# A transformer block on one core: the last two groups of the down projection issued as one

## The reference, cut to what matters

```python
for l in range(DEPTH):                       # DEPTH = 1, x is (1, 1024, 1024) float32
    h = rms_norm(x, g_mix[l])
    ...                                      # attention and mLSTM heads give mix
    x = x + mix @ w_out[l]
    h2 = rms_norm(x, g_ffn[l])
    x = x + (silu(h2 @ w_gate[l]) * (h2 @ w_up[l])) @ w_down[l]     # D_FF = 2816
```

## Time and profile before

| | |
|---|---|
| median of 3 runs | 1052.51 us (1050.98 to 1052.51) |
| the profiled execution, its own time | 1053.27 us |
| its span, first to last instruction | 1051.5 us |
| PE busy | 1022.6 us (97%) |
| DVE, POOL, ACT busy | 683.3, 707.2, 432.0 us |
| mean granted clock of TensorE | 0.988 |

### The profile page before, as it was taken

How to read it: one execution, slowest core, us unless ns; L and a number is a source line. 1 busy time by engine, 2 the same in 40 slices (tenths; PEclk the granted TensorE clock), 3 DMA queues, 4 the chain that set the end, 5 groups by cost and what they waited for, 6 DMA issues and landing times.

```text
span 1051.5 us, 13511 instructions
## 1 busy us (share of the span) xinstructions
PE 1022.6 (97%) x4970; PEld 841.0 (80%) x4970; DVE 683.3 (65%) x790; ACT 432.0 (41%) x895; POOL 707.2 (67%) x555
## 2 busy tenths in 40 slices
PE   9999999999989997999999999999999999999978
PEld 7898878878878876888888888888888888888856
DVE  4259359857752579474858676675858585766386
ACT  7545124357740556533434252434334342524420
POOL 0138578825655337978778687786887786878872
PEclk9999999999999998999999999999999999999988
DMA  7123212131032001111211212112112112121104
GB/s 232 56 61 89 72 41 61 61 130 32 21 122 60 20 11 51 60 50 41 81 41 44 78 41 66 55 41 80 40 41 81 41 50 72 41 70 51 41 30 160
DMA packets 71162, 66.06 MB, mean 63 GB/s; under 512 B 5305, under 2 KB 53689, under 8 KB 71097
## 3 DMA queue, kind: packets, MB, share of 16 engines
q1 hardware_dynamic: 70104, 64.71, 19.8%
q10 hardware_dynamic: 992, 0.49, 0.2%
HBM read 60.48 MB, written 4.21 MB: 62 GB/s over the span
## 4 chain that ended last, share of the span: by engine, by line
PE 73%; DVE 17%; issue 4%; ACT 3%; POOL 2%; DMA 0%; POOLq 0%; SPq 0%; DVEq 0%; ACTq 0%
PE banks L759 23%; PE banks L761 22%; PE banks L760 22%; DVE af_lo L1905 7%; DVE af_raw L1896 2%; DVE af_raw L1898 2%; ACT prob L1391 1%; PE banks L779 1%; DVE sg L1884 1%; PE banks L845 1%; POOL wr_lo L698 1%; DVE af_raw L1887 1%; DVE af_raw L1901 1%; DVE prob L1828 1%; DVE smx L1833 1%
## 5 line engine op out<-in xcount | busy, mean ns | idle before, releaser
L698 POOL TENSOR_TENSOR wr_lo<-wr_raw,wr_hi 128x512 fp32r<-128x512 f32 x231 | 315.0, 1392 | 38.4 <-ACT wr_hi L1221 33.3
L692 POOL TENSOR_TENSOR wr_raw<-wr_raw,wr_raw 128x512 f32<-128x512 f32 x132 | 191.0, 1451 | 130.0 <-PE banks L761 115.4
L759 PE MATMUL banks<-hf_hi,wr_hi 128*128 128x512 f32 x616 | 243.0, 394 | 6.9 <-issue 2.7
L761 PE MATMUL banks<-hf_hi,wr_lo 128*128 128x512 f32 x616 | 241.5, 392 | 0.0
L760 PE MATMUL banks<-hf_lo,wr_hi 128*128 128x512 f32 x616 | 241.3, 392 | 0.0
L1983 DVE TENSOR_TENSOR x<-banks,x 128x1024 f32<-128x1024 f32 x154 | 188.2, 1224 | 61.4 <-PE banks L761 46.5
L1221 ACT ACTIVATE wr_hi<-wr_raw 128x512 fp32r<-128x512 f32 x231 | 136.9, 625 | 159.4 <-POOL wr_raw L692 101.5
L759 PE MATMUL banks<-w_hi,actT_hi 128*128 128x512 f32 (+1 forms) x448 | 173.1, 386 | 1.5 <-DVE x L1792 1.5
L760 PE MATMUL banks<-w_lo,actT_hi 128*128 128x512 f32 (+1 forms) x448 | 168.6, 376 | 0.0
L761 PE MATMUL banks<-w_hi,actT_lo 128*128 128x512 f32 (+1 forms) x448 | 168.5, 376 | 0.0
L759 PEld LDWEIGHTS banks<-hf_hi,wr_hi 128*128 128x128 f32 x616 | 116.4, 189 | 36.2 <-DVE sg L1884 4.4
(11 more groups left out here) (201 smaller groups left out, 1236.1 us busy)
## 6 DMA issues: line engine op xcount, KB each, us to landing
wr_raw<-in_w_up SPq DMA_DIRECT2D x46, 256.0 KB, 3.4
wr_raw<-in_w_gate SPq DMA_DIRECT2D x44, 256.0 KB, 3.3
wr_raw<-in_w_down SPq DMA_DIRECT2D x44, 256.0 KB, 3.1
w_raw<-in_w_in SPq DMA_DIRECT2D x32, 256.0 KB, 3.5
w_raw<-in_w_out SPq DMA_DIRECT2D x16, 256.0 KB, 2.6
x<-in_x SPq DMA_DIRECT2D x8, 512.0 KB, 6.2
out<-x SPq DMA_DIRECT2D x16, 256.0 KB, 2.2
x_in<-in_x SPq DMA_DIRECT2D x7, 512.0 KB, 4.3
```

The source lines that it names most:

```text
L692: nc.gpsimd.tensor_tensor(wr_raw[slot(q, f)][:, :], wr_raw[slot(q, a)][:, :], wr_raw[slot(q, b)][:, :], ALU.subtract).then_inc(wsum, 1)
L698: nc.gpsimd.tensor_tensor(wr_lo[s][:, :], wr_raw[s][:, :], wr_hi[s][:, :].bitcast(F32), ALU.subtract).then_inc(wf_lo, 1)
L759: nc.tensor.matmul(ps, x_hi, wh, start=first, stop=False, skip_group_check=more)
L761: return nc.tensor.matmul(ps, x_lo, wh, start=False, stop=last, skip_group_check=more)
```

## The change

Five things change, all in the last two down stages, down 9 (QA) and down 10 (QB).

The order of TensorE: products are issued as 1 of QA, 2 of QA, 1 of QB, 2 of QB, and then form by form, QA's and QB's product of a form behind each other (`LAST_PRODUCTS`, `down_pair`). Both accumulate in the same banks and VectorE adds them once, so 14 adds of 128x1024 go; the last form is added bank by bank (`dve_last`).

The place of QB's weights: seven slots of their own, in space of the normalised tokens' forms 6 and 5, which no product reads any more once forms 6 and 5 of up 10 are done. Their loads and sums wait for that instead of for slots.

The low parts of the last activations: made by VectorE between its adds, not by GpSimd at the end; those of forms 1 and 2 in a place of their own, ahead of the sums.

The order of ScalarE and GpSimd in these two stages: hand-written lists that alternate QA and QB (`LAST_HIGH`, `LAST_LOWS`, `LAST_SUMS`), with functions that give each its count.

The stores: the last four wait for one add each.

```diff
+        DEAD6 = [M0 + 2 * SIDE, M0 + 2 * SIDE + SLOT, W0 + 2 * SIDE, W0 + 2 * SIDE + SLOT]
+        DEAD5 = [M0 + 3 * SIDE, M0 + 3 * SIDE + SLOT, M1]
+        LAST_LOW = M1 + SLOT
...
+        first_dead = len(UPPER + LOWER)
+        SLOTS.append({f: first_dead + i for i, f in enumerate((1, 2, 7, 3, 5, 6, 4))})
...
+        LAST_PRODUCTS = [(QA, 1), (QA, 2), (QB, 1), (QB, 2)] + [(q, f) for f in FORMS[2:] for q in (QA, QB)]
...
         def slot_free(engine, q, f):
+            if q == QB:
+                engine.wait_ge(gu_done, product(GU["up", JS - 1], 5 if f in (5, 6, 4) else 6))
...
+            def down_pair(j):
+                for q, f in LAST_PRODUCTS:
+                    n, b = at_form(f), q - QA
+                    first = {1: 0, 6: 0, 7: 0, 4: 0}.get(f, 4)
+                    pe.wait_ge(wf_lo, low_count(q, f))
+                    pe.wait_ge(act_lo_s, 7 * (j + b) + n + 1)
+                    s = slot(q, f)
+                    new = b == 0 and f in (1, 2, 5)
+                    for t in range(4):
+                        if b == 0 and t % 2 == 0:
+                            if n >= 2:
+                                pe.wait_ge(down_add, 14 * j + 2 * n - 3 + t // 2)
...
+                        last = three(bank[first + t][:, :], af_hi[b][f][:, a], af_lo[b][f][:, a],
+                                     wr_hi[s][:, :], wr_lo[s][:, :], new, b == 1, f not in (1, 2, 5))
+                        if b == 1 and (t % 2 == 1 or f == FORMS[-1]):
+                            last.then_inc(dn_done, 1)
...
+            def act_last():
+                for q, f in LAST_HIGH[2:7]:
+                    weight_high(q, f)
+                for f in A_HI[:3]:
+                    act_high(JS - 1, {1: 1, 2: 2, 4: 4}[f])
...
+            def dve_last(j):
+                act_low(JS - 1, 1)
+                act_sums(JS - 1, 1)
+                dve.wait_ge(act_raw, 8 * JS)
+                for n, f in enumerate(FORMS[:-1]):
+                    add_down(j, n, f)
+                    if n + 2 < len(FORMS):
+                        act_low(JS - 1, FORMS[n + 2])
+                dve.wait_ge(down_add, 14 * j + 12)
+                for t in range(4):
+                    dve.wait_ge(dn_done, 14 * j + 12 + t + 1)
+                    xs = x1[:, 4 + t, 0:N]
+                    V_.tensor_tensor(xs, bank[t][:, :], xs, ALU.add).then_inc(down_add, 1)
```

More of the change, by code:

```diff
@@ L614, in _ @@
             for t in range(4):
-                store(4 + t, 0, 13 + t // 2)
+                store(4 + t, 0, 13 + t)
             sp.wait_ge(out_s, 16 * 2 * T)
@@ L707, in fourth_sum @@
                                         ALU.subtract).then_inc(h2_s4, 1)
-            for q in range(NQ):
+            for q in range(QA):
                 n = 16 * (q // 2 + 1)
@@ L746, in _ @@
                     block_low(q, f)
[L747 to L752, removed]
+            for q in (QA, QB):
+                n = 16 * (q // 2 + 1)
+                pool.wait_ge(b11_s[q % 2], n)
+                pool.wait_ge(b12_s[q % 2], n)
+                block_sum(q, 5, 7, 1)
+                pool.wait_ge(wsum, sum_count(q, 5))
+                block_low(q, 1)
+                pool.wait_ge(b22_s[q % 2], n)
+                block_sum(q, 6, 3, 5)
+                pool.wait_ge(wsum, sum_count(q, 6))
+                pool.wait_ge(b21_s[q % 2], n)
+                block_sum(q, 4, 2, 6)
+                pool.wait_ge(wsum, sum_count(q, 4))
+                block_low(q, 2)
+            for f in (6, 5):
+                block_low(QA, f)
+                block_low(QB, f)
+            for q in (QA, QB):
+                block_sum(q, 7, 3, 7)
+            pool.wait_ge(wsum, sum_count(QB, 7))
+            for f in (7, 3, 4):
+                block_low(QA, f)
+                block_low(QB, f)
         @block.tensor
@@ L1501, in act_down @@
             def act_down(q, j):
[L1502 to L1507, removed]
+                for f in FORMS:
+                    weight_high(q + 1, f)
             act_first()
@@ L1516, in _ @@
                     act_up(q, j)
-                else:
+                elif q < QA:
                     act_down(q, j)
+                elif q == QA:
+                    act_last()
         @block.vector
@@ L1969, in dve_first, with add_down @@
                 gated(0, 0, 2, af_raw[0][2])
+            def add_down(j, n, f):
+                rows = 0 if f in (1, 2, 6, 3) else 4
+                half = {1: 0, 2: 0, 6: 1, 3: 1, 5: 1, 7: 1, 4: 0}[f]
+                first = 0 if f in (1, 6, 7, 4) else 2
+                for h in range(2):
+                    dve.wait_ge(dn_done, 14 * j + 2 * n + h + 1)
+                    if n >= 1 or j >= 1:
+                        dve.wait_ge(down_add, 14 * j + 2 * n + h - 1)
+                    xs = x1[:, rows + 2 * h:rows + 2 * h + 2, half * N:(half + 1) * N]
+                    V_.tensor_tensor(xs, banks[first + h][:, :, :], xs, ALU.add).then_inc(down_add, 1)
             def dve_down(j):
[L1972 to L1973 removed]
                 for n, f in enumerate(FORMS):
[L1975 to L1978, removed]
[L1979 to L1983 removed]
+                    add_down(j, n, f)
[4 more added lines that the diff above has]
+                for n, f in enumerate(FORMS[:-1]):
+                    add_down(j, n, f)
+                    if n + 2 < len(FORMS):
[5 more added lines that the diff above has]
+                    V_.tensor_tensor(xs, bank[t][:, :], xs, ALU.add).then_inc(down_add, 1)
             dve_first()
```

68 lines of the change are left out of this document (52 added, 16 removed).

## The result

The changed kernel takes 1039.89 us (median of 4 runs, 1039.06 to 1041.04), the kernel before 1051.98 us in the same comparison (4 runs). The ratio is 0.9885, 95% interval 0.9874 to 0.9897: 12.1 us less. Forecast were 1041.6 and a range of 1039.2 to 1044.5. The profiled execution took 1039.53 us, its span is 1037.7.

A forecast was written before the change was run, and what follows sets the result against it. PE, busy 97% of the span, was taken as the bound. Last matmul end at 1037.1 plus a 3.5 us tail gave 1040.6 against 1051.5, 10.9 us less; forecast median 1041.6 us, range 1039.2 to 1044.5.

The forecast's parts named there:

- The two old waits: TensorE's waits in down 9 and 10, 2.2 and 4.9 us, would go, with half clocks costing 1.7 and 2.3.
- The new wait: TensorE waits for VectorE ahead of the fifth and sixth products, 1.4 us in all, bounds 0 and 3.0.
- rival A: The forecast itself for the whole kernel: 1041.6 us, own range 1040.3 to 1043.0, chance 0.60.
- rival C: VectorE keeps up because GpSimd gives it more turns than priced: 1.4 us less, 1040.2, chance 0.12.
- What 168 matmuls need: Joined down 9 and 10 take 0.230 us per matmul, 167 steps from 996.91, ending at 1035.7 without waits.
- The new wait ahead of the fifth product: TensorE waits 1.1 us for VectorE's first add, behind low parts, a gate product and four sums taking 11.1 us.
- The clock behind the new wait: Waits of 1.1 and 0.3 us in the joined stages cause no clock loss; a drop would cost 1.7 us.
- Rival B: The clock falls behind the new wait in the joined stages: 1.7 us more, 1043.3, chance 0.15.
- The weights in time: Down 10's loads start at 986.1, GpSimd's first sum at 994.3; weights arrive before use, smallest slack 2.7 us.
- Rivals D and E: A weight or activation part late, 1044.5 to 1048, chance 0.08; down 10's loads not early, slower than before, chance 0.02.
- GpSimd rid of seven low parts: GpSimd drops seven low parts, 8.7 us, the first being what TensorE waited 4.9 us for.
- The tail: From last matmul to end of span, a one-bank add and single store take 3.5 us instead of 4.45.

The follow-up runs named there:

- operands on one side: Changed kernel with high and low parts of the last activations moved to the lower addresses, beside down 10's weights; 1039.07 us, ratio 0.9881 to the kernel before.
- low parts ahead: Changed kernel with the low part of form 6, or of forms 6 and 5, made before VectorE's first add; 1042.66 and 1046.18 us.
- quiet GpSimd: Changed kernel with GpSimd setting five low parts of weights to zero instead of computing them; 1039.69 us in one run.
- dead space alone: Kernel before with only down 10's weights given seven slots in the space of token forms 6 and 5; 1045.62 us, ratio 0.9945.
- low parts on VectorE alone: Kernel before with only the seven low parts of the last activations moved from GpSimd to VectorE; 1047.36 us, ratio 0.9955.
- both without the join: Kernel before with low parts on VectorE and down 10's weights in dead token space, stages still in sequence; 1048.97 us, ratio 0.9967.

## Why the prediction was right, step by step

**What was right, and what was luck.** The two old waits and both half clocks went, as forecast, and they are most of the 12.1 us. The new wait, put at 1.4 us, came to 0.17, so that the time fell below the bounds of the forecast itself (rival A) and is closest to rival C, which had been given a chance of 0.12. About half a microsecond of that is not the change's: the kernel before took 1051.98 us beside the changed one, and the forecast had started from 1052.51; the gain was 12.1 us where 10.9 were forecast. Rival C's reason holds in part only: the low parts of forms 2 and 6 were cheap, while all four sums cost 1.67 to 1.79 us, as forecast. From the start of the pair to the end of the last matmul 40.2 us were forecast and 39.2 measured, and the tail brought 0.3 more.

**What 168 matmuls need.** Forecast 38.8 us at 0.230, between two paces that I could not choose from. Measured are both paces in turn, 0.2267 in down 9's products from form 5 on and 0.233 in down 10's, and that their cause is the place of the activations is shown by the kernel with operands on one side. With the wait of 0.17 taken off, the pair needs 39.0.

**The new wait ahead of the fifth product.** The mechanism was right (VectorE's chain up to the first add, shown by the kernels with low parts ahead), the size was not: 1.1 forecast and 0.17 measured, and 0.3 ahead of the sixth where there is none. This is the term that was mis-sized. The chain took 1005.24 - 994.89 = 10.35 us and not 11.1. The low part of form 2 cost 1.18 and not 1.77; instructions start up to 0.1 before the one ahead has ended in the records, so their durations can't simply be added. The two adds took 2.36 together, and TensorE came 0.1 us later than I had put it, by its slower pace. Low part 6 then cost 0.68 where I had 1.77. I had priced every low part at the median; beside a busy GpSimd a single one behind an add cost anything from 0.68 to 1.79, and I take it to depend on where GpSimd stands in its own instruction when VectorE's starts. The SBUF page of the Trainium skill (Terms) has it that the loser of the shared port pair is blocked for a full instruction of the other; the three prices 0.68, 1.18 and 1.79 of one operation, and 0.69 beside a quiet GpSimd, agree with that in kind. In size they stay below it: 0.68 and a full 1.29 of GpSimd's would be 1.97 for either engine, and the most in these stages of the changed kernel is 1.79 for VectorE and 1.77 for GpSimd.

**The clock behind the new wait.** No loss, as forecast, but a wait of 0.17 us does not test what was forecast of one of 1.1. Rival B's way exists: behind 3.26 us the clock fell. Behind 1.59 it stayed in the one profile that there is, and behind the wait of 1.87 to 1.90 us at 304 it fell in seven profiles and stayed in five. So the length of the wait alone does not decide, and the comparison of 1.49 with 1.90 us from one trace was a thinner ground than it looked.

**The weights in time.** Right. The loads of down 10 start at 984.60, 10.7 us ahead of the start of the pair (forecast 986.1, 10.8 ahead), and GpSimd's first sum for down 10 at 993.14, 2.2 us ahead of it (forecast 994.3, 2.6 ahead). The smallest slack was a little overstated: five of GpSimd's instructions at 1.7 us from 994.3 end at 1002.8 and not 1002.5, which leaves 2.4 us instead of 2.7. Measured are 2.4: the low part of the weights' form 2 ends at 1001.25, and its product starts at 1003.63. Rivals D and E did not happen.

**GpSimd rid of seven low parts.** I put the whole 4.9 us wait down to them. The runs correct the reason: dead space alone removes that wait too, with the low parts still on GpSimd at the end, and in the joint order their engine is worth 0.5 us. What had made them late was that GpSimd could not begin down 10's weights before down 9's products freed the slots.

**The tail.** 3.5 instead of 4.45 forecast, 3.2 measured. The step took its gain from the shorter add and the single store; what was larger than I put down is the time from the last store's issue to the end of the span, 2.44 instead of 2.74 us.

**Where the 12.1 us came from**, by subtraction of pairs and tails: dead space 6.0; the joint order 4.4 (44.1 to 39.7, low parts on GpSimd in both, though they stand elsewhere in its list); low parts on VectorE 0.5; single last adds and stores 1.2. The order of subtraction matters: low parts on VectorE alone would be worth 6.1, and both without the join less than either. The joint order without the dead space was not tried, since a slot that down 10's form 6 needs would be freed by a product that is issued behind it.

## What to carry to other kernels

When the last two groups of work stand behind each other, look whether the second's preparation waits for storage that the first frees; storage that died earlier, for another reason, is worth as much as a faster engine, and the two gains do not add. Joining both groups' products of a form in one accumulation halves the reads and gives the engine that reads them time at the very place where it is late. Before moving work to an engine, check what its neighbour does at that moment: a gap in GpSimd's work, made by a wait elsewhere, can be what kept VectorE fast.

## What the runs showed of the hardware

A 128x512 TENSOR_TENSOR of VectorE within SBUF costs 0.68 us when GpSimd does not compute. Beside a computing GpSimd the four sums in a row cost 1.67 to 1.79 each, and a single low part behind an add between 0.68 and 1.79. A read of PSUM, 1.23 for 128x1024, is the same either way. A matmul of 128x512 whose two operands lie on different sides of the address space (one below 140,000 bytes of a partition, the other above 177,000) is followed by the next 6.6 ns later than one with both on one side, 0.2333 against 0.2267 us, seen in down 10's products from form 6 on in each profile and gone when one operand was moved; where between the two addresses the border lies was not tried. A wait of TensorE of 1.9 us was followed by 3.4 us at half clock in seven of twelve profiles and by none in the other five; behind the six waits of 2.2 us and more in the last two stages of these profiles the clock fell every time. Between two executions of the changed kernel this moved the start of the last two stages by 1.4 us (996.73 and 995.30).
